# Load, first norm and gates inside the block of the DeltaNet layer

## What is computed

```python
def rmsnorm(x, w):
    y = xf * lax.rsqrt(jnp.mean(xf * xf, axis=-1, keepdims=True) + RMS_EPS)
    return (y * w)

def gdn_mixer(x, S0, conv_buf, chunk, w_in, conv_w, A_log, dt_bias, norm_w, w_out):
    h = x @ w_in                                   # x is the normed input
    qkv, z, b, a = jnp.split(h, [GDN_QKV, z_end, z_end + GDN_HEADS], axis=-1)
    qkv, new_buf = causal_short_conv(qkv, conv_buf, conv_w)
    ...
    beta = jax.nn.sigmoid(b)
    log_a = -jnp.exp(A_log) * jax.nn.softplus(a + dt_bias)
```

## Time and profile before

| | us |
|---|---|
| median of 3 runs | 4231.16 (4229.22 to 4231.58) |
| the profiled execution | 4229.97 |
| its span, first to last instruction | 4228.3 |
| PE busy | 3884.9 (92%) |
| DVE busy | 1797.5 (43%) |
| POOL busy | 1180.8 (28%) |
| ACT busy | 919.7 (22%) |

### The profile page before, as it was taken

How to read it: one execution, slowest core, us unless ns; L and a number is a source line. 1 busy time by engine, 2 the same in 40 slices (tenths; PEclk the granted TensorE clock), 3 DMA queues, 4 the chain that set the end, 5 groups by cost and what they waited for, 6 DMA issues and landing times. The chain is left out here.

```text
span 4228.3 us, 55001 instructions
## 1 busy us (share of the span) xinstructions
PE 3884.9 (92%) x20398; PEld 2980.4 (70%) x20398; DVE 1797.5 (43%) x3022; ACT 919.7 (22%) x2068; POOL 1180.8 (28%) x998
## 2 busy tenths in 40 slices
PE   5799989999789999999999968999989999999999
PEld 4466666666666888888876656666657688888887
DVE  3255654455545111116661023666646411111666
ACT  1223333323311000000000002555542100100001
POOL 0012111122122233323330002566643233332332
PEclk7899999999879999999999979999999999999999
DMA  1201111101033111114311130000013311111422
GB/s 59 89 26 37 40 36 30 36 25 36 11 104 99 40 40 40 40 44 127 94 39 40 59 110 1 1 1 1 1 42 95 96 40 40 40 40 44 131 83 77
DMA packets 321326, 215.03 MB, mean 51 GB/s; under 512 B 28266, under 2 KB 312931, under 8 KB 319523
## 3 DMA queue, kind: packets, MB, share of 16 engines
q1 hardware_dynamic: 315670, 206.14, 16.5%
q0 software_dynamic: 2048, 5.25, 0.4%
q10 hardware_dynamic: 3456, 1.57, 0.2%
HBM read 187.08 MB, written 29.91 MB: 51 GB/s over the span
## 5 line engine op out<-in xcount | busy, mean ns | idle before, releaser
L862 PE MATMUL ps<-xT,work 128*128 128x272 f32 x2688 | 644.6, 393 | 0.0
L862 PEld LDWEIGHTS ps<-xT,work 128*128 128x128 f32 x2688 | 511.6, 190 | 105.8
L1351 PE MATMUL ps<-xn,work 128*128 128x363 f32 (+1 forms) x1536 | 550.5, 478 | 24.4 <-DMA work<-in_gdn_w_in_dram 17.6
L862 PE MATMUL ps<-xn,work 128*128 128x272 f32 x2016 | 490.5, 393 | 3.9 <-DVE work L933 3.9
L862 PEld LDWEIGHTS ps<-xn,work 128*128 128x128 f32 x2016 | 383.0, 190 | 84.0 <-issue 5.1
L476 PE MATMUL ps<-work 128*128 128x272 f32 x1676 | 403.2, 397 | 11.5 <-PEq L830 4.3
L476 PEld LDWEIGHTS ps<-work 128*128 128x128 f32 x1676 | 321.1, 192 | 82.4 <-issue 15.9
L2712 POOL TENSOR_SCALAR work<-work 128x640 f32<-128x640 f32 (+4 forms) x192 | 314.0, 1646 | 196.4 <-DVE work L2615 196.0
L1351 PEld LDWEIGHTS ps<-xn,work 128*128 128x128 f32 x1536 | 262.5, 192 | 122.5 <-issue 38.4
L735 POOL TENSOR_TENSOR xT<-xT,work 128x272 f32<-128x272 f32 x96 | 198.4, 2080 | 265.6 <-DVE work L601 167.2
L1900 POOL TENSOR_TENSOR xT<-xT,consts 128x512 f32<-128x512 f32 x96 | 136.9, 1439 | 452.2 <-DVEq L1745 384.6
(11 more groups left out here) (401 smaller groups left out, 5669.6 us busy)
## 6 DMA issues: line engine op xcount, KB each, us to landing
work<-in_ffn_w_in_dram SPq DMA_DIRECT2D x88, 512.0 KB, 5.0
xn<-in_ffn_w_out_dram SPq DMA_DIRECT2D x46, 704.0 KB, 4.7
work<-in_gdn_w_in_dram SPq DMA_DIRECT2D x32, 512.0 KB, 4.2
work<-in_ffn_w_out_dram SPq DMA_DIRECT2D x18, 704.0 KB, 4.6
ffn_parked_residual<-xT SPq DMA_DIRECT2D x2, 4352.0 KB, 13.8
work<-in_gdn_w_out_dram SPq DMA_DIRECT2D x32, 256.0 KB, 2.9
work<-in_nsa_w_out_dram SPq DMA_DIRECT2D x64, 128.0 KB, 2.9
xT<-ffn_parked_residual SPq DMA_DIRECT2D x4, 1632.0 KB, 9.2
```

The costliest lines, as they stand in the source:

```text
L862: ins = pe.matmul(acc(a, n), w[:, k, :], t[:, k, a * SUB:(a + 1) * SUB], start=(first and k == 0), stop=(k == HK - 1), skip_group_check=True)
L1351: mm = pe.matmul(unit_acc(u, m), w[j % 2][:, k, :], c.xn[:, k, o:o + cnt], start=(k == 0), stop=(k == KD - 1))
```

## The change

`load_stage`, `norm_stage` and `gate_stage` are gone; their work stands at the head of each engine's program in the block of `gdn_stage`, without barriers between.

- Tokens come by tiles of 128 (first the 64 sample tokens, then the 8 prompt tiles), each with its own semaphore. Only the first 259 columns of constants are loaded ahead; the others, the page table and the parking come later in SP's order. ACT issues the five vector loads.
- The squares of a tile are summed on ACT ahead of the transposition, with the accumulating output of one Square over 1024 features; then root and reciprocal of one column per tile. PE spreads the 128 scales over all partitions with a matmul against the identity, and DVE norms the tile in 8 steps of 128 columns with the scales read from PSUM.
- Each tile's 8 transpositions fill two PSUM banks; ACT copies one half out, DVE the other.
- The gates' products are made with `wba` as weights and 363 columns of `c.xn` moving, 8 matmuls for each of the three column ranges. The first 8 are split over tiles 6 and 7 of the loop; the others follow the last tile. The result (16 rows) is copied out by ACT and turned by PE inside the first projection, after its first unit; the sums of log_a come after its second, the turning of the rows after its third.
- On SP the row stores, the wait for them and the spread rows stand behind the first weights and ahead of the reload for the third tile.

```diff
@@ SP
+                sp.dma_start(c.ct[:, 0:EARLY], io["consts"][:, 0:EARLY]).then_inc(early, 16)
+                for t in order:
+                    tokens = io["x_prompt"][0][t * P:(t + 1) * P, :] if t < NC else io["x_sample"].rearrange("b t d -> (b t) d")
+                    sp.dma_start(rows[t], tokens).then_inc(xl[t], 16)
+                sp.dma_start(wba, w_in[:, :, 4096:4112]).then_inc(gil, 16)
...
+                sp.dma_start(cv, io["state_gdn_conv"][0].rearrange("b r f -> (b r) f")).then_inc(cvl, 16)
                 for j in range(2):
                     sp.dma_start(w[j], w_in[:, :, j * D:j * D + P]).then_inc(wl[j], 16)
+                sp.dma_start(c.ct[:, EARLY:], io["consts"][:, EARLY:]).then_inc(late, 16)
+                sp.dma_start(c.pages[:, :], io["page_table"].rearrange("b (o n) -> o (b n)", o=1)).then_inc(late, 16)
+                sp.wait_ge(xc0, 9)
+                sp.wait_ge(xc1, 9)
+                sp.dma_start(park, c.xTf).then_inc(parked, 16)
                 sp.dma_start(s0.rearrange("p (b v) -> p b v", b=NB), io["state_gdn"][0][:, 0].rearrange("b k v -> k b v")).then_inc(s0l, 16)
+                sp.wait_ge(rk, 1)
+                for x_ in range(2):
+                    sp.dma_start(c.gate_rows[x_].rearrange("h (c t) -> (h c) t", c=9), gate_out[0:72, x_ * P:(x_ + 1) * P]).then_inc(rst, 16)
+                sp.wait_ge(rst, 32)
                 sp.wait_ge(parked, 16)
@@ PE
-                pe.wait_ge(parked, 16)
+                def turn_tile(n, t):
+                    pe.wait_ge(xl[t], 16)
+                    if n >= 2:
+                        pe.wait_ge(xc0, n - 1)
+                        pe.wait_ge(xc1, n - 1)
+                    for k in range(KD):
+                        mm = pe.transpose(turned(n, t, k // 4)[:, k % 4, :], rows[t][:, k * P:(k + 1) * P],
+                                          const(c, "ident")[0:height(t), 0:height(t)])
...
+                def spread_scales(n, t):
+                    h = height(t)
+                    pe.wait_ge(ivd, n + 1)
+                    if n >= 2:
+                        pe.wait_ge(xnd, n - 1)
+                    pe.matmul(spread(n, t), inv9[0:h, t:t + 1].to_broadcast([h, P]), const(c, "ident")[0:h, 0:h],
+                              start=True, stop=True).then_inc(bcd, 1)
+
+                def gate_product(m, ks, tiles):
+                    o, cnt = CH[m]
+                    pe.wait_ge(gil, 48)
+                    pe.wait_ge(xnd, tiles)
+                    for k in ks:
+                        mm = pe.matmul(bank(c, (6, 7, 5)[m])[0:16, 0:cnt], wba[:, k, :], c.xn[:, k, o:o + cnt],
+                                       start=(k == 0), stop=(k == KD - 1))
...
-                for _ in stream(0, True):
+                pe.wait_ge(early, 16)
+                for n, t in enumerate(order):
+                    turn_tile(n, t)
+                    if n == 0:
+                        turn_vectors()
+                    else:
+                        spread_scales(n - 1, order[n - 1])
+                    if n == 6:
+                        gate_product(0, range(4), 4)
+                    elif n == 7:
+                        gate_product(0, range(4, KD), 4)
+                spread_scales(8, order[8])
+                turn_conv_rows()
+                gate_product(1, range(KD), 7)
+                gate_product(2, range(KD), 9)
+                pe.matmul(bank(c, 4)[:, 480:496], const(c, "ones")[0:1, :], row[0:1, :], start=True, stop=True)
+                pe.wait_ge(gcp, 2)
+                first = stream(0, True)
+                for units, then in ((1, turn_gates), (1, gate_sums), (1, turn_gate_rows)):
+                    for _ in range(units * UNIT):
+                        next(first)
+                    then()
+                for _ in first:
                     pass
@@ ACT
+                def tile_root(n, t):
+                    h = height(t)
+                    act.wait_ge(xl[t], 16)
+                    act.activation(squares_out[0:h, :], rows[t], ACT.Square, accum_out=ssum[0:h, t:t + 1]).then_inc(sqs, 1)
+                    act.wait_ge(sqs, n + 1)
+                    act.activation(rts[0:h, t:t + 1], ssum[0:h, t:t + 1], ACT.Sqrt, bias=const(c, "eps")[0:h, :], scale=1.0 / D).then_inc(rtd, 1)
+
+                def keep_half(n, t):
+                    act.wait_ge(tr, 2 * n + 1)
+                    act.activation(c.xT[:, 0:4, tile_cols(t)], turned(n, t, 0), ACT.Copy).then_inc(xc0, 1)
...
+                act.wait_ge(early, 16)
+                act.activation(junk1, const(c, "eps"), ACT.Sqrt)
+                for n, t in enumerate(order):
+                    tile_root(n, t)
+                    keep_half(n, t)
+                for m in range(3):
+                    act.wait_ge(gpr, m + 1)
+                    act.activation(gate_in[:, CH[m][0]:CH[m][0] + CH[m][1]], bank(c, (6, 7, 5)[m])[0:16, 0:CH[m][1]], ACT.Copy).then_inc(gcp, 1)
                 for j in range(3):
                     for m in range(3):
                         take_unit(0, j, m, True)
+                        if (j, m) == (0, 0):
+                            gate_logs()
+                        elif (j, m) == (0, 2):
+                            gate_exps()
@@ DVE
+                def norm_tile(n, t):
+                    dve.wait_ge(vk, 1)
+                    dve.wait_ge(bcd, n + 1)
+                    dve.wait_ge(xc0, n + 1)
+                    dve.wait_ge(xc1, n + 1)
+                    for k in range(KD):
+                        ins = dve.scalar_tensor_tensor(out=c.xn[:, k, tile_cols(t)], in0=c.xT[:, k, tile_cols(t)], scalar=c.normw[:, k:k + 1],
+                                                       in1=spread(n, t), op0=ALU.mult, op1=ALU.mult)
+                    ins.then_inc(xnd, 1)
...
+                for n, t in enumerate(order):
+                    if n == 1:
+                        keep_vectors()
+                    invert_tile(n, t)
+                    keep_half(n, t)
+                    if n:
+                        norm_tile(n - 1, order[n - 1])
+                norm_tile(8, order[8])
+                keep_conv_rows()
...
+                gates()
+                dve.wait_ge(late, 32)
```

More of the change, by code:

```diff
@@ L56, in const_table @@
     add("ones", np.ones((P, P)))
+    add("eps", np.full((P, 1), EPS))
+    add("eps_dk", np.full((P, 1), EPS * P))
+    add("one", np.ones((P, 1)))
     add("upper", i <= j)
@@ L79, in const_table @@
     add("s_far_add", np.where(k8 >= t, 0, NEG))
-    add("eps", np.full((P, 1), EPS))
-    add("eps_dk", np.full((P, 1), EPS * P))
-    add("one", np.ones((P, 1)))
     return np.concatenate(cols, 1)
@@ L1206, in gdn_stage, with temp, by_chunk, tile_cols @@
     sn, um = lt[:, 0:NB * P], ml[:, 0:NB * P]
+    order = [NC] + list(range(NC))
+    rows = [yT[:, t * D:(t + 1) * D] for t in range(NC)] + [kt[0:NS, 0:D]]
+    ssum, rts, inv9, junk1 = kt[:, D:D + 9], kt[:, D + 9:D + 18], kt[:, D + 18:D + 27], kt[:, D + 27:D + 28]
+    squares_out = c.work[:, 2 * D:3 * D]
+    cv = c.work[0:24, nxt_at:nxt_at + QKV]
+    vec1, vec2 = us[0:41, :], us2_[0:96, :]
+    at = [0]
+    def temp(n):
+        a = bv[:, at[0]:at[0] + n]
+        at[0] += n
+        return a
+    wba = temp(KD * 16).rearrange("p (k f) -> p k f", k=KD)
+    row, rb = temp(16), temp(16)
+    ba, t1, t2, t3, gsum, tot, by_head, gate_out = temp(144), temp(72), temp(72), temp(72), temp(72), temp(72), temp(144), temp(2 * P)
+    assert at[0] <= 9 * P, at[0]
+    gate_in = bb[0:16, :]
+    parv = c.par.rearrange("p (h q c) -> p q c h", h=HG, q=6)
+    ba3 = ba.rearrange("p (c n) -> p c n", c=9)
+    def by_chunk(a):
+        return a.rearrange("p (c h) -> p c h", c=9)
+    def tile_cols(t):
+        return slice(t * P, t * P + (P if t < NC else NS))
+    def height(t):
+        return P if t < NC else NS
+    def turned(n, t, half):
+        return bank(c, 2 * (n % 2) + half)[:, 0:4 * height(t)].rearrange("p (k t) -> p k t", k=4)
+    def spread(n, t):
+        return bank(c, 4 + n % 2)[:, 0:height(t)]
     park = nc.dram_tensor("parked_residual", (P, KD * NT), F32).ap()
@@ new lines, in turn_gates, with gate_sums @@
+                def turn_gates():
+                    pe.wait_ge(gcp, 3)
+                    for t in range(9):
+                        mm = pe.transpose(bank(c, 0)[0:height(t), 16 * t:16 * t + 16], gate_in[:, tile_cols(t)], const(c, "ident")[0:16, 0:16])
+                    mm.then_inc(pm, 1)
+                def gate_sums():
+                    pe.wait_ge(late, 32)
+                    pe.wait_ge(step, 8)
+                    la, las = t3[:, 0:64], t3[0:NS, 64:72]
+                    pe.matmul(bank(c, 1)[:, 0:64], const(c, "upper"), la, start=True, stop=True)
+                    pe.matmul(bank(c, 1)[0:NS, 64:72], const(c, "upper_s")[0:NS, :], las, start=True, stop=True)
+                    pe.matmul(bank(c, 1)[:, 128:192], const(c, "ones"), la, start=True, stop=True)
```

(6 more changed lines are left out.)

288 lines of the change are left out of this document (101 added, 187 removed).

## The result

The changed kernel takes 4138.97 us (median of 4 runs, 4134.17 to 4139.6) against 4231.37 (4 runs, 4229.22 to 4235.87): a ratio of 0.9778, 95% interval 0.9766 to 0.9789. The forecast was 4140.7, range 4128 to 4158. The profiled execution took 4134.17, its span is 4132.5.

A forecast was written before the change was run, and what follows sets the result against it. Until 137.2 us engines work mostly in turn; behind that PE bounds the kernel. Starting the first projection at 46.2 us saves 91.0, gate steps inside add 0.5: -90.5 from 4231.16 gives 4140.7 us, range 4128 to 4158.

The forecast's parts named there:

- Load and first tile: At the start: sample tokens in at about 3.5 us, first prompt tile at 4.7, DVE's copy of the vectors 0.5.
- Pace: In the tile loop: DVE sets the pace with 3.03 us per full tile, bounds 2.6 to 3.4.
- Gate halves: Between tiles 6 to 8: two halves of the first gate product delay PE by nothing to 4.2 us, taken as 1.2.
- Conv turns and products: Behind the last tile on PE: 24 conv transposes 2.7 us, two gate products 9.7 at the full clock.
- The clock: Ahead of the first projection: PE starts from the lower clock, costing 2.7 us once.
- Inside the projection: Gates' steps within the first projection: 3.2 us, less 2.7 its first unit no longer loses, so +0.5.
- early: Rival for the stretch up to the first projection: pace 2.6 and PE never cold, projection at 39, total 4133; chance 0.12.
- Cold all the way: Rival on PE: gate halves, conv turns, last gate products and first projection unit all cold, +13.6 us, 4154; chance 0.11.
- Vectors late: Rival at the first norm: five small loads land behind all tokens and DVE waits, +11.5 us, 4152; chance 0.05.
- tables reloaded: Rival in the tile loop: ACT reloads tables at each tile, needs 4.7 us and passes DVE, +17, 4158; chance 0.03.
- not really beside: Rival in the first projection: the gates' chain isn't covered or third weights come late, +8 us, 4149; chance 0.04.
- The slower one: Rival: PE stays at the lower clock through first projection and into head 0, 4240 or more; chance 0.03, 0.02 of it slower.

The follow-up runs named there:

- dve_both: Changed kernel with DVE copying both halves of every turned tile out of PSUM and ACT none; 4142.43 us.
- again_2: Changed kernel run once more without edit, as the measure for other runs on its chip; median 4135.61 us (5 runs).
- gates_ahead: Changed kernel with all small steps of the gates ahead of the first projection instead of inside it; 4146.42 us.
- again: Changed kernel run once more without edit, to see its own spread; median 4134.65 us (4 runs).
- gates_token_weights: Changed kernel with the gates' products in the old form (token tiles as weights, 16 columns moving, 72 matmuls) behind the last tile; 4161.1 us.
- gates_behind_tiles: Changed kernel with the first gate product behind all tiles with the other two, not between tiles 6 to 8; 4142.93 us.
- gates_alone: Changed kernel with loading and first norm as separate stages again, only the gates moved into the block; 4191.34 us against 4232.74 for the kernel before.
- combined: Changed kernel with ACT copying both halves, vectors turned later, sample tile last and gate products earlier; 4134.85 us against 4135.61 for the changed kernel.
- tables: Changed kernel with an unused one-column Exp behind each tile's Sqrt, so ACT loads two tables per tile; 4153.29 us (one run).
- load_ahead: Changed kernel with PE and ACT waiting for all nine token transfers before the first tile; 4145.74 us.
- act_both: Changed kernel with ACT copying both halves of every turned tile, DVE only inverting and norming; 4136.09 us.
- vectors_later: Changed kernel with PE turning the five vectors behind the first prompt tile instead of ahead of it; 4136.62 us (one run).

## Why the prediction held

The mechanism held: DVE set the pace of the tiles, the gates' products in their new form ran at the full clock, and the rest lay beside the projection. That the time was right to 1.7 us is more than its terms earned: they were off by up to 2.7 us each, and the errors partly cancelled. By its own steps:

- **Load and first tile.** Sample tokens came at 5.55, not 3.5, and PE stood 1.5 us for the vectors ahead of the first prompt tile. I had priced DVE's copy of them and not PE's wait, though PE turns them ahead of that tile in the code. The first norm group began at 11.36, 2.5 late.
- **Pace.** 2.72 instead of 3.03, inside the bounds. The mean durations of the rows overlap in the queue: DVE's copy of 0.67 starts 0.07 after the start of a reciprocal of 0.16. (The prediction's bounds take the change of pace eight times, its sum has seven such steps; that is 0.4 us of its range.) dve_both and the row of stages show that DVE was the one to count.
- **Gate halves.** No delay in the profiled execution instead of 1.2; 1.7 in again_2 (some 0.3 of it a later start of the tiles), 3 in gates_ahead. The bounds were right, the value is a matter of where the clock stands.
- **Conv turns and products.** 1.6 and 9.9, for 2.7 and 9.7.
- **The clock.** The 2.7 us did not come, and this is the one wrong reading; its rows stand behind this list.
- **Inside the projection.** 0.7 for the turns, 0.77 of waiting for the sums (0.8 forecast), 1.1 and 0.3 for sums and rows: 70.1 us instead of the 69.8 forecast. The third weights were issued 21.4 us after the projection's start and waited for by nobody.
- **Sum.** First projection 42.1 for 46.2, of which +2.5 and -2.2 (start, pace), -1.2 (halves), -1.1 (conv turns), -2.7 (clock) and +0.6 in the rest. So head 0 started at 112.3 instead of the forecast 116.0. Behind it the profiled execution was 1.6 us faster than before, where no change was forecast, and so it came out 5.3 us below its forecast of 4139.5. The median is only 1.7 below, because it lies 4.8 above the profiled execution; the forecast had carried over the 1.2 of the kernel before. That part is luck: against the medians of again and again_2 the miss would be some 6 and 5 us.

**The wrong reading, in rows.** The sum let PE come cold to its projection matmuls, whichever came first, as at 137.2 before. What PE had done ahead of them was the evidence to use, and that is here the turning of tiles: in the earlier trace rows it took 421 ns per transpose at first and 328 later. In the changed kernel transposes from 8.7 to 12.7 took 421 ns each, and from 13.3 on 273. The first row below, the transposes of a 128-token tile grouped by source line (count, least/median/most ns of one, from when to when), the second the same line from 13.3 on, still ahead of any gate product:

```profile
L1193 PE MATMUL ps<-consts,work x8: 421/421/422, 8.7 to 10.2; 128*128 128x128 f32 x8
...
L1193 PE MATMUL ps<-consts,work x14: 272/273/273, 13.3 to 15.0; 128*128 128x128 f32 x14
```

PE had done nothing but these light steps of the tiles by then, and the clock stayed up until the gate products. That 421 ns belong to the lower clock can be seen where it is on record; this row of dve_both lies in its stretch at 0.50 (19.1 to 25.9):

```profile
L1193 PE MATMUL ps<-consts,work x8: 417/417/445, 21.2 to 22.8; 128*128 128x128 f32 x8
```
The Trainium skill (TensorE: Matmul & The Clock Gate, Part 4: PE-mode transpose) says that full clock does not engage in transpose mode; for float32 transposes these rows, like the earlier trace rows, show that it does. The prediction weighed the rule and held with the row, and then still counted a cold start. The opposite rule, that turning tiles keeps the clock up, doesn't follow either: in gates_token_weights, gates_behind_tiles and dve_both it fell while PE did nothing but these steps. The prediction misplaced one such fall. It put the fall before into the stage that sums squares (from 38.18), but the clock is at 0.50 from 36.2 on, while PE was still turning convolution rows and vectors without a pause (12 records in the 1.60 us from 36.20 to 37.80).

Of the rivals, "early" came nearest, with PE never cold from 13.3 on and a pace of 2.72 for its 2.6; it priced the projection at 39, and the start, 2.5 later than summed, and the slower pace make most of the 3 us up to 42.1. "Cold all the way" was seen in no profile of the changed kernel, though again_2 had its first half cold. "Vectors late" was true in small (1.5 us, not 11.5), "tables reloaded" was tried and costs 19 at the projection for the 17 that were said, and "not really beside" was tried in gates_ahead, where the chain costs 8.6 for the 8 that were said. The slower one, a clock that stays down through the projection and into head 0, showed nowhere: no projection here took over 72 us.

**What I can't settle.** The loop of heads, from head 0's first turn to head 7's last, takes 892.3 us in the changed kernel and 889.3 before (112.3 to 1004.6 and 206.5 to 1095.8). In the clock's records it has short falls to 0.50. One of them, with a little of the full clock at its edges (changed kernel, columns as in the earlier trace rows):

```profile
153.50:156.90 3.40, 3.40 (x14) 2.65 (x13) 1.75 (x5) 0.00 (x0) 0.34 (x1) 0.53 0.93 271
```

| kernel | falls of 3.4 us in the loop (one of 6.8 counts as two) | loop, us |
|---|---|---|
| gates_alone | 8 | 889.0 |
| before | 9 | 889.3 |
| combined, tables, load_ahead, gates_behind_tiles | 9 | 890.5 to 890.8 |
| changed, again, again_2, gates_ahead, gates_token_weights, dve_both, act_both, vectors_later | 10 | 892.2 to 892.5 |

Half the clock over 3.4 us is up to 1.7 us of work, and over all 14 profiles the time goes with the count. The cause of the count I only argue: the loop has a pause of PE in each head, and how the falls meet it may depend on when the loop starts; no run here tells that. So 94.2 us gained ahead of the heads are some 91 at their end. The profiled execution still ends 95.8 earlier, so 4.6 come back behind the heads; as again shows, the same kernel varies by as much there, and I don't count them to the change.

## What to carry to other kernels

Stages in which one engine after the other is busy can shrink towards the time of the engine with the most work, if the tile that is handed on is small enough for that engine to start early; here 137 us became 42. Once the engines overlap, ask which one has no pause left and from when: relieving DVE by 0.6 us a tile moved the first projection by 1.4, because PE was full from its first gate product on. Matmuls with many moving columns are well placed between light PE work that has pauses: with them behind it the projection stood 7.3 us later here, some 3 of it by the clock.

## What the runs showed of the hardware

- With 16 moving columns behind each 128x128 weight load, PE was busy for 18.00 of 18.00 us (42 to 60 in gates_token_weights), and the granted clock was 0.50 in all of them. In the changed kernel it had risen by 13.3 (421 to 273 ns per transpose) when PE had only turned tiles and spread scales, busy for 4.19 of the 5.81 us ahead of the first norm group. Under the same kind of work it fell at 19.1, 26.9 and 29.3 in three of the runs.
- A clock of 1.00 in rows ahead of the first change on record does not tell the level here: transposes took 421 ns in such a stretch (8.7 to 10.2 in the changed kernel) and 417 where 0.50 is on record (dve_both, 21.2 to 22.8); the durations tell.
- The gates' last input, a load of a few bytes, came at 18.0 us in combined, behind 4.5 MB on its queue, of which the last token tile had landed at 17.5.
- Five loads issued by ACT, 69 KB in all, were there when PE's wait for them ended at 8.3 us, with tokens at full rate on SP's queue beside them (402 GB/s from 5.55 to 11.36); in the kernel before, on SP's queue behind the tokens, they had landed at 20.7.
